# Projections with stationary weights: hi and lo halves accumulated in one 256-column region instead of a 512-column one

## What is computed

```python
h = rms_norm(x, g_mix); proj = h @ w_in          # 2048 -> qa, ka, va, qr, kr, vr, gr, gates
...                                              # block attention, retention, gates, w_out
g, u = jnp.split(h2 @ w_ffn_in, 2, axis=-1)
x = x + (silu(g) * u) @ w_ffn_out                # first layer done
h = rmsnorm(x, attn_pre_norm); proj = h @ w_in_2 # gq, gk, gv, gg, ga, dq, dk, dv
...                                              # gated linear attention, differential attention, w_o
up = h @ w_ffn_in_2; a, b = up[..., :5632], up[..., 5632:]
a = causal 3-tap convolution of a over the rows + bias
x = x + rmsnorm((gelu(a) * b) @ w_ffn_out_2)
```

## Time and profile before

| | |
|---|---|
| median of three runs | 2815.34 us |
| their range | 2813.99 to 2817.28 us |
| profiled execution, first to last instruction | 2817.5 us |
| TensorE matmul busy | 2758.4 us (98%) |
| TensorE weight loads busy, beside matmuls | 2301.1 us (82%) |
| VectorE busy | 1601.3 us (57%) |
| ScalarE busy | 1309.7 us (46%) |
| mean granted TensorE clock | 0.993 of full speed |

### The profile page before, as it was taken

One profiled execution on the slowest core, in us unless ns is written; L12 is line 12 of the kernel. 1 busy time (PEld: TensorE's weight loads), 2 busy tenths in 40 slices (PEclk: granted clock), 3 DMA queues, 4 the chain that ended last, 5 costly groups with the idle time before them and its releaser, 6 DMA issues.

```text
span 2817.5 us, 37249 instructions
## 1 busy us (share of the span) xinstructions
PE 2758.4 (98%) x13311; PEld 2301.1 (82%) x13311; DVE 1601.3 (57%) x1636; ACT 1309.7 (46%) x1544; POOL 89.7 (3%) x61
## 2 busy tenths in 40 slices
PE   7999999999999999999999999998999999999997
PEld 6887778788888888888888888777778888888886
DVE  4557655545555444444454555576676666666444
ACT  5435555454445444444444443454554444444443
POOL 0000000000000000000000000121000000000000
PEclk9999999999999999999999999999999999999999
DMA  6665555566666666666566665543456666665554
GB/s 221 190 187 161 161 171 164 167 201 215 190 188 181 190 190 187 192 187 192 186 193 192 188 177 172 158 138 108 162 168 186 185 185 184 188 186 188 193 193 141
DMA packets 231189, 507.65 MB, mean 180 GB/s; under 512 B 15653, under 2 KB 15877, under 8 KB 230084
## 3 DMA queue, kind: packets, MB, share of 16 engines
q1 hardware_dynamic: 229616, 499.31, 58.7%
q0 software_dynamic: 1360, 7.21, 0.8%
q10 hardware_dynamic: 132, 0.03, 0.0%
HBM read 504.39 MB, written 2.10 MB: 180 GB/s over the span
## 4 chain that ended last, share of the span: by engine, by line
PE 94%; ACT 2%; DVE 2%; issue 1%; DMA 0%; DVEq 0%; SPq 0%; ACTq 0%
PE ps L341 21%; PE ps L343 20%; PE ps L342 20%; PE ps L333 19%; PE ps L334 9%; PE ps L405 1%; ACT whi L761 1%; PE ps L664 1%; PE ps L656 0%; DVE wlo L1206 0%; DMA raw<-w_in 0%; PE ps L597 0%; PE ps L439 0%; PE ps L718 0%; PE ps L502 0%
## 5 line engine op out<-in xcount | busy, mean ns | idle before, releaser
L1206 DVE TENSOR_TENSOR wlo<-raw,whi 128x1024 fp32r<-128x1024 f32 x944 | 1171.4, 1242 | 1133.4 <-ACT whi L761 1126.2
L761 ACT ACTIVATE whi<-raw 128x1024 fp32r<-128x1024 f32 x944 | 1000.2, 1060 | 1432.2 <-PE ps L343 991.0
L333 PE MATMUL ps<-hT,whi 128*128 128x512 f32 x2304 | 817.3, 400 | 5.9 <-DVE hT L1254 5.9
L341 PE MATMUL ps<-whi,hT 128*128 128x512 f32 x1792 | 715.4, 399 | 7.4 <-ACT big L860 2.4
L343 PE MATMUL ps<-whi,hT 128*128 128x512 f32 x1792 | 701.5, 391 | 0.0
L342 PE MATMUL ps<-wlo,hT 128*128 128x512 f32 x1792 | 700.9, 391 | 0.0
L334 PE MATMUL ps<-hT,wlo 128*128 128x256 f32 x2304 | 646.9, 281 | 0.0
L333 PEld LDWEIGHTS ps<-hT,whi 128*128 128x128 f32 x2304 | 434.7, 189 | 113.7 <-DVE hT L1254 7.6
L334 PEld LDWEIGHTS ps<-hT,wlo 128*128 128x128 f32 x2304 | 436.7, 190 | 0.1
L341 PEld LDWEIGHTS ps<-whi,hT 128*128 128x128 f32 x1792 | 338.5, 189 | 80.2 <-issue 2.9
L343 PEld LDWEIGHTS ps<-whi,hT 128*128 128x128 f32 x1792 | 338.4, 189 | 72.0
(11 more groups left out here) (232 smaller groups left out, 1060.7 us busy)
## 6 DMA issues: line engine op xcount, KB each, us to landing
raw<-w_ffn_in SPq DMA_DIRECT2D x352, 512.0 KB, 3.6
raw<-w_in SPq DMA_DIRECT2D x304, 512.0 KB, 3.8
raw<-w_ffn_out SPq DMA_DIRECT2D x176, 512.0 KB, 4.3
raw<-w_o_ret SPq DMA_DIRECT2D x32, 512.0 KB, 4.6
raw<-w_out SPq DMA_DIRECT2D x32, 512.0 KB, 4.6
raw<-w_o SPq DMA_DIRECT2D x32, 512.0 KB, 3.6
raw<-w_o_attn SPq DMA_DIRECT2D x16, 512.0 KB, 4.6
resid<-x SPq DMA_DIRECT2D x2, 1024.0 KB, 6.4
```

Source lines behind the costliest of these rows:

```text
L333: pe.matmul(acc, whi[:, c % SLOTS, f], hT[:, kt, :, :], start=(kt == 0), stop=False)
L341: pe.matmul(acc, hi, whi[:, c % SLOTS, f], start=start, stop=False)
L761: act.activation(whi[:, c % SLOTS, :], raw[:, c % SLOTS, :], ACT.Copy).then_inc(hi_ready, 1)
L1206: dve.tensor_tensor(wlo[:, c % SLOTS, :], raw[:, c % SLOTS, :], whi[:, c % SLOTS, :].bitcast(F32), ALU.subtract).then_inc(lo_ready, 1)
```

## The change

In `cols_block` the pair becomes three matmuls of 256 columns, all into the same 256-column half of a bank; two tiles `ft` share a bank, and a block takes two banks: 0 and 1 for `par` 0, 2 and 3 for `par` 1. The product `ga` is changed in the same way and goes to bank 4. ScalarE's copy and VectorE's add are taken out; VectorE scales straight from PSUM. The wait in `head_norms` and the one ahead of `ga` are taken out. Sections behind `ga` swap their two bank pairs, and the last section `fo2` starts with banks 4 to 7. Cut to its core:

```diff
                         for ft in range(tiles):
-                            acc = ps[:, 4 * par + ft, :]
+                            acc = ps[:, 2 * par + ft // 2, ft % 2 * SEQ:ft % 2 * SEQ + SEQ]
                             f = slice(k2 * 512 + ft * P, k2 * 512 + ft * P + P)
-                            pe.matmul(acc, whi[:, c % SLOTS, f], hT[:, kt, :, :], start=(kt == 0), stop=False)
-                            mm = pe.matmul(acc[:, 0:SEQ], wlo[:, c % SLOTS, f], hT[:, kt, 0, :], start=False,
-                                           stop=(kt == KT - 1))
+                            first, last = kt == 0 and ft % 2 == 0, kt == KT - 1 and ft % 2 == 1
+                            pe.matmul(acc, whi[:, c % SLOTS, f], hT[:, kt, 0, :], start=first, stop=False)
+                            pe.matmul(acc, whi[:, c % SLOTS, f], hT[:, kt, 1, :], start=False, stop=False)
+                            mm = pe.matmul(acc, wlo[:, c % SLOTS, f], hT[:, kt, 0, :], start=False, stop=last)
...
             def head_norms(pos):
-                if pos == 0:
-                    pe.wait_ge(acc_freed, base["va"] + 1)
                 if pos % 4 == 1:
...
-            pe.wait_ge(acc_freed, base["gv"])
             for kt in range(KT):
                 f = slice(kt * 16, kt * 16 + P)
-                pe.matmul(ps[:, 0, :], ga_hi[:, f], hT[:, kt, :, :], start=(kt == 0), stop=False)
-                mm = pe.matmul(ps[:, 0, 0:SEQ], ga_lo[:, f], hT[:, kt, 0, :], start=False, stop=(kt == KT - 1))
+                pe.matmul(ps[:, 4, 0:SEQ], ga_hi[:, f], hT[:, kt, 0, :], start=(kt == 0), stop=False)
+                pe.matmul(ps[:, 4, 0:SEQ], ga_hi[:, f], hT[:, kt, 1, :], start=False, stop=False)
+                mm = pe.matmul(ps[:, 4, 0:SEQ], ga_lo[:, f], hT[:, kt, 0, :], start=False, stop=(kt == KT - 1))
...
-            def low_sums(blk, par):
-                block_done(blk)
-                act.wait_ge(acc_freed, blk + 1)
-                act.activation(lo_sum.rearrange("p (f t) -> p f t", f=4), ps[:, 4 * par:4 * par + 4, SEQ:], ACT.Copy)\
-                    .then_inc(lo_copied, 1)
...
-            def add_low(blk, par, nth, dst):
-
-                dve.wait_ge(lo_copied, nth + 1)
-                return dve.tensor_tensor(dst, ps[:, 4 * par:4 * par + 4, 0:SEQ], lo_sum.rearrange("p (f t) -> p f t", f=4), ALU.add)
...
-            def scaled(x):
-
-                return dve.tensor_tensor(x, x, scale_row.rearrange("p (f t) -> p f t", f=1).to_broadcast([P, 4, SEQ]), ALU.mult)
+            def scaled_tiles(blk, par, dst):
+
+                block_done(blk)
+                return dve.tensor_tensor(dst, ps[:, 2 * par:2 * par + 2, :].rearrange("p b (f t) -> p (b f) t", f=2),
+                                         scale_row.rearrange("p (f t) -> p f t", f=1).to_broadcast([P, 4, SEQ]), ALU.mult)
```

More of the change, by code:

```diff
@@ L555, in _, with feed_out @@
                 rows_block(base["out"] + n, n % 2, turned=None if n else S("turned2"), side=out_side, x=merged)
-            def feed_out(name, u, last_side=nothing, first_side=nothing, rows_before=False):
+            def feed_out(name, u, last_side=nothing, first_side=nothing, rows_before=False, bank0=0):
                 b = base[name]
@@ L640, in _ @@
                     pe.wait_ge(S("g_ga"), 1)
-                rows_block(base["gv"] + n, 1 - n, side=low_rank if n else nothing)
+                rows_block(base["gv"] + n, n, side=low_rank if n else nothing)
             ke, qe = area_g[:, 0:LW], area_g[:, LW:2 * LW]
@@ L745, in _ @@
             pairs("ff2", 2 * FBLK, cols_block, first_side=turn_ahead(6, resid), turned=S("turned6"))
-            feed_out("fo2", 1)
+            feed_out("fo2", 1, bank0=4)
         @block.scalar
@@ L851, in _ @@
             act.wait_ge(S("eps_ok"), 1)
-            pairs("qk", 4, lambda blk, par, i: low_sums(blk, par), first_side=turn_ahead(0, GAIN["mix"], 2, range(4)))
-            pairs("qkr", 4, lambda blk, par, i: low_sums(blk, par))
+            pairs("qk", 4, no_epilogue, first_side=turn_ahead(0, GAIN["mix"], 2, range(4)))
+            pairs("qkr", 4, no_epilogue)
             def late_rows(dst, func):
@@ L1060, in _ @@
                 ahead(base["gv"] + n, low_rank if n else nothing)
[L1061 removed]
+                late_rows(gv, ACT.Copy)(base["gv"] + n, n, n)
             decays = free_c[:, 0:9 * P]
@@ L1093, in _ @@
                     ahead(base[section] + n, side)
-                    rows(base[section] + n, 1 - n, n)
+                    rows(base[section] + n, n, n)
             dT, s_both = temp[:, 1024:1536], area_g[:, 0:1024]
@@ L1318, in _, with keep_tiles @@
                 split(0, c)
-            def keep_tiles(dst, nth0):
+            def keep_tiles(dst):
                 def epilogue(blk, par, i):
-                    tiles = dst[:, bass.ds(4 * i, 4), :]
-                    own(add_low(blk, par, nth0 + i, tiles))
-                    scaled(tiles).then_inc(acc_freed, 1)
+                    scaled_tiles(blk, par, dst[:, bass.ds(4 * i, 4), :]).then_inc(acc_freed, 1)
                 return epilogue
@@ L1330, in _ @@
             s1, on = temp[:, 0:512], temp[:, 1536:1792]
-            pairs("qk", 4, keep_tiles(tiles_a, 0), first_side=turn_ahead(0, GAIN["mix"], 2), per=1)
-            pairs("qkr", 4, keep_tiles(tiles_b, 4), per=1)
-            n_cols = 8
+            pairs("qk", 4, keep_tiles(tiles_a), first_side=turn_ahead(0, GAIN["mix"], 2))
+            pairs("qkr", 4, keep_tiles(tiles_b))
             def head_tiles(h):
@@ L1502, in stage, with feed_in @@
                                   staged[:, buf, :, 0, :].bitcast(F32), ALU.subtract).then_inc(S(f"staged{u}"), 1)
-            def feed_in(name, u, first_side, gate_sum, per, side2, n_cols):
+            def feed_in(name, u, first_side, gate_sum, per, side2):
                 b = base[name]
@@ L1585, in _ @@
             held(base["fo"] + FBLK - 1)
-            pairs("gqk", 2, keep_tiles(tiles_b, n_cols), first_side=turn_ahead(4, GAIN["pre2"], 4), per=1)
+            pairs("gqk", 2, keep_tiles(tiles_b), first_side=turn_ahead(4, GAIN["pre2"], 4))
             dve.wait_ge(S("ga_hi"), 1)
@@ L1591, in _ @@
                 .then_inc(S("ga_lo"), 1)
-            pairs("dqk", 4, keep_tiles(tiles_a, n_cols + 2), per=1)
-            n_cols += 6
-            dve.wait_ge(lo_copied, n_cols + 1)
-            own(dve.tensor_tensor(temp[0:16, 0:SEQ], ps[0:16, 0, 0:SEQ], lo_sum[0:16, 0:SEQ], ALU.add))
-            own(dve.tensor_tensor(temp[0:16, 0:SEQ], temp[0:16, 0:SEQ], scale_row[0:16, :], ALU.mult))
-            dve.sem_inc(S("g_ga"), 1)
-            n_cols += 1
+            pairs("dqk", 4, keep_tiles(tiles_a))
+            dve.wait_ge(S("ga_mm"), 1)
+            dve.tensor_tensor(temp[0:16, 0:SEQ], ps[0:16, 4, 0:SEQ], scale_row[0:16, :], ALU.mult).then_inc(S("g_ga"), 1)
             log_a = temp[:, 1024:2048]
@@ L1789, in post_norm, with conv_sum @@
                     ins.then_inc(S("norm_in6"), 1)
-            def conv_sum(blk, i, nth):
-                own(add_low(blk, 0, nth, conv_in[:, :, 2:]))
+            def conv_sum(blk):
+                own(scaled_tiles(blk, 0, conv_in[:, :, 2:]))
                 dve.sem_inc(acc_freed, 1)
-                own(scaled(conv_in[:, :, 2:]))
             def convolve(tap, i):
@@ L1812, in convolve @@
                     ins.then_inc(S("conv_done"), 1)
-            feed_in("ff2", 1, turn_ahead(6, GAIN["ffn2"], 0, post_norm), conv_sum, 5, convolve, n_cols)
+            feed_in("ff2", 1, turn_ahead(6, GAIN["ffn2"], 0, post_norm), conv_sum, 3, convolve)
             def out_gain(q):
                 dve.wait_ge(S("norm_part8"), q + 1)
-                own(dve.tensor_tensor(rows_a[:, :, q * 512:q * 512 + 512], ps[:, 2 * q:2 * q + 2, :], row_gain(q), ALU.mult))
+                own(dve.tensor_tensor(rows_a[:, :, q * 512:q * 512 + 512], ps[:, (2 * q + 4) % 8:(2 * q + 4) % 8 + 2, :], row_gain(q),
+                                      ALU.mult))
             def out_gains(k):
```

25 lines of the change are left out of this document (9 added, 16 removed).

## The result

| | before | changed |
|---|---|---|
| median | 2813.99 us (5 runs, 2807.13 to 2817.28) | **2831.33 us** (5 runs, 2828.98 to 2833.77) |
| profiled execution | 2817.5 us | 2832.0 us |

The ratio is 1.0065, with a 95% interval of 1.0044 to 1.0087: the change makes the kernel 0.65% slower. Forecast were 2829.6 us and +0.5%, and for the profiled execution 2831.7.

What follows compares the result with a forecast made beforehand. TensorE's matmul stream was taken as the bound: 2817.5 + 18.8 (added matmuls) - 1.2 (absorbed waits) - 3.4 ("va") = 2831.7 us profiled, less the 2.2 us offset to the median 2829.6 us, +0.5%; range 2802 to 2848 us.

Steps and rivals of the forecast that it cites:

- The price of a triple: Changed blocks: three 256-column matmuls cost 360.0 ns, 120.0 each, against pairs of 346.6 or 353.4; together +18.8 us.
- rival 1: Changed blocks: the added matmul is nearly free, 115 to 116 ns per 256-column matmul, kernel faster at 2803 us; chance 0.17.
- rival 2: Changed blocks: only a small fixed cost, 1 to 3 ns, for the second whi pass, 2817 us; chance 0.12.
- 366.7: Later sections: rival price in ns of a triple if the extra 6.7 ns remain on top, 2841 us; chance 0.15.
- 380: Everywhere: rival price in ns of a triple if the later price holds for each matmul, 2874 us; chance 0.08.
- The 6.7 ns of "ff2": Old pairs in "ff2" cost 353.4 ns against 346.6 in "qk", 6.7 more for the same instructions, no cause found.
- The start of "va": Start of "va": old bank wait of 2.1 us goes, a wait of about 0.6 for the squares comes; -3.4 us.
- the last step: End of the sum: profiled span lies 2.2 us over the runs' median; carried over, 2831.7 becomes 2829.6 us.
- its term for the slow clock: Start of "va": about 1.6 of the 3.4 us gained is the slow clock, if the shorter pause doesn't set it off.
- the sign given to look for: In "va": L439 about 2.7 us or less behind the second chunk's start.
- The absorbed 1.2 us: First blocks of "qk", "gqk", "ff2": added matmul time shortens TensorE's waits for the scale row at L418; -1.2 us.
- The epilogues: Ends of 36 blocks: removing ScalarE's copy and VectorE's add takes 44 us from VectorE, worth nothing outside "va".

Runs made afterwards that it cites:

- b_halves: Kernel before, with only the 512-column matmul of each pair split into two of 256 columns, one per bank half; 2836.83 us, ratio 1.0074.
- c_grouped: Kernel before, with four 512-column matmuls first and then four of 256 for each kt; 2814.49 us, ratio 1.0004.
- d_full512: Kernel before, with the 256-column matmul widened to 512, so lo x lo is computed too; 3047.63 us.
- i_384: Kernel before, with both matmuls of a pair at 384 columns (first at kt 0 keeps 512), part of the product missing; 2812.97 us, ratio 0.9995.
- h_alternate: Changed kernel, with the three matmuls ordered whi x hi, wlo x hi, whi x lo; 2830.56 us, ratio 1.0063.

## Why the prediction was right

**The price of a triple**, the term that carries the sum: forecast 360.0 ns, measured 360.0 in all three sections and again in two variants. The way to it, a window's count for the 512-column matmul and the difference in a pair for the 256-column one, held, and so did the choice of the evenly running stream as the neighbour to go by. Streams of 384 and of 512 columns alone show the same 13.3 ns. All four rivals fell with the window of "ff2": at 345 to 348 ns a triple (rival 1), 356 (rival 2), 366.7 or 380 it would have held another count than 3335.

The Trainium skill ("TensorE: Matmul & The Clock Gate", section "Wait — 56ns, not 53.3ns?") has a fixed cost of about 2.5 ns a matmul at the fast clock. That isn't what fp32r matmuls pay here: it is 13.3 ns at three lengths, and the measurement decides.

**The 6.7 ns of "ff2"**: the sum took the two levels of the trace as fixed, +6.9 in "qk" and +11.8 in the rest. The terms are right for that one execution: 2831.7 us forecast, 2832.0 measured. Had the trace been one with all sections low, the same terms would have given +30.7 - 4.6 on a span of 2817.5 - 12.0 = 2805.5: 2831.6, the same end by a larger loss, since the changed kernel's stream is steady. What isn't safe is the last step. It takes the distance of the trace's span from the median of the runs before, 2.2 us, for the same after the change; measured after it are 2832.0 - 2831.33 = 0.7, and that is nearly all of the 1.7 us by which the median was missed. From the low trace the same step would have added 9.8 us and ended near 2841. That this trace lay so near the median was luck. The loss against the kernel before is what varies by execution, between 13.4 and 6.7 ns a unit.

**The start of "va"**: -3.4 forecast, 3.61 - 6.95 = -3.34 measured in the traces, the new wait 0.5 instead of 0.6 us, late for the reason given (ScalarE's chunk 4, then the squares). The size of its term for the slow clock held (1.6 us forecast, 1.59 measured). But the slow clock doesn't always follow that pause: b_halves, c_grouped and d_full512 have the same pause and no slow clock. So the change saves 1.75 us where the clock would have stayed up and 3.34 where it would not. Two of the prediction's readings here are off without touching the sum. The nine matmuls of the earlier trace rows are about eight, since 3.40 us hold eight at 427 ns. And the sign given to look for, L439 about 2.7 us behind the start of the second chunk, doesn't fit its own 207.3 - 203.95 = 3.35; measured are 213.26 - 209.88 = 3.38.

**The absorbed 1.2 us**: the mechanism of this term is the wrong one, though its size came out near. The waits for the scale row went from 2.7 to 2.3 us, 0.4 in place of 1.2, and the one in "qk", where 0.6 was to be absorbed, stayed at 1.2. (The four waits for `hT` went from 5.9 to 6.2, which says nothing: the second trace of the kernel before has 7.5.) The stretch of "qk" and "qkr" nevertheless grew by only 5.84 us in place of 6.9. Two things of the clock come in. At the slow clock the fixed cost doesn't show, for the first few us; and in the changed kernel's trace the fast clock came more than 1 us sooner, which by the halved pace is worth an estimated 0.6 us. Before, near the start:

```profile
17.04 0.63 PE L333 MATMUL ps<-hT,whi 128*128 128x512 f32 x1
...
17.68 0.63 PE L333 MATMUL ps<-hT,whi 128*128 128x512 f32 x1
...
22.17 0.47 PE L333 MATMUL ps<-hT,whi 128*128 128x512 f32 x1
22.48 0.28 PE L334 MATMUL ps<-hT,wlo 128*128 128x256 f32 x1
```

and in the changed kernel:

```profile
17.14 0.41 PE L332 MATMUL ps<-hT,whi 128*128 128x256 f32 x1
...
17.78 0.41 PE L332 MATMUL ps<-hT,whi 128*128 128x256 f32 x1
...
20.55 0.38 PE L333 MATMUL ps<-hT,whi 128*128 128x256 f32 x1
20.76 0.28 PE L334 MATMUL ps<-hT,wlo 128*128 128x256 f32 x1
```

0.64 us for 768 columns both times, 768 / 1.2 GHz and nothing more. (The start of "ff2", where the windows 2060.00:2063.00 before and 2065.00:2068.60 after print a clock of 0.50, has the same 0.64 in both.) A 256-column matmul is recorded at 0.41 us at the slow clock and at 0.28 at the fast one, a 512-column one at 0.63 and 0.40. So the clock rose in the matmul at 22.17 us (0.47) before and in the one at 20.55 us (0.38) in the changed kernel. Whether the change has a part in that isn't shown.

**The sum by stretches** of the two traces, each from its first matmul to the first of the next (before: 16.24, 201.20, 1609.45, 1754.47, 2059.41 us and the last matmul at 2802.84; changed: 16.33, 207.13, 1612.13, 1759.72, 2064.84 and 2817.42):

| stretch | before | changed | difference | forecast |
|---|---|---|---|---|
| "qk" and "qkr" | 184.96 us | 190.80 us | +5.84 | 6.9 - 0.6 |
| "va" up to "gqk" | 1408.25 | 1405.00 | -3.25 | -3.4 |
| "gqk", "dqk", `ga` | 145.02 | 147.59 | +2.57 | 2.5 + 0.1 - 0.3 |
| behind `ga` up to "ff2" | 304.94 | 305.12 | +0.18 | 0 |
| "ff2" to the last matmul | 743.43 | 752.58 | +9.15 | 9.3 - 0.3 |

So the sum holds stretch by stretch, and not only at its end.

**The epilogues**: worth nothing, as forecast, except at "va". VectorE's busy time fell by 35 us instead of the 44 forecast: 36 adds of 1.22 us went, but the 944 splits are recorded 8 ns longer each (1250 against 1242). The only wait of TensorE that named copy or add is the one at "va", and b_halves, which has them all, has the same 360.0.

## What to carry to other kernels

Where TensorE is the bound, count matmuls as well as columns: splitting one fp32r matmul of 512 columns in two costs 13.3 ns each time in streams of one length. Against the mixed pairs of this kernel it was 13.3 or 6.7 ns, 2304 times over, and work saved on engines that nobody waits for doesn't pay for it. Take the price of an instruction from counts in windows without gaps and from streams like the new one, not from recorded durations or from single distances in a mixed stream. And take more than one trace of the kernel before when its runs spread as much as the effect looked for: here the trace's own stretches differed by 6.7 ns a pair for the same code.

## What the runs showed of the hardware

- In streams of one length, an fp32r matmul at the granted clock of 1.00 (2.4 GHz) starts columns / 2.4 + 13.3 ns after the last: 120.0, 173.3 and 226.7 ns for 256, 384 and 512 columns. At 1.2 GHz (start of "ff2", granted clock 0.50) 768 columns take 0.64 us in two matmuls or three, with no fixed cost to be seen.
- With 128 columns it is 111.6 ns at 2.4 GHz, where that formula has 66.7, and 214 ns at 1.2 GHz. Something that isn't the columns sets the pace there, and it follows the array's clock.
- Streams that alternate 512 and 256 columns ran at 346.7 or 353.3 ns a pair in each section of three traces, and the level of a section can differ between two executions of the same kernel. Four and four gave 350.9, two and two 348.7 in "ff2". What picks the level isn't known.
- The pause of 2.1 us in "va" was followed by a granted clock of 0.5 in the kernel before (two traces) and in i_384, and by none in b_halves, c_grouped and d_full512.
- A tile of weights used by two matmuls in a row is loaded twice (15631 loads for 15631 matmuls), and changing the order so that it isn't used twice in a row costs nothing (h_alternate).
